# A decoder trunk on one core: score levels as two 64-column tiles, convolution taps dealt out anew, modulation sums behind each step's evacuation

## What is computed

```python
def step(state, inp):                       # recurrence, chunk by chunk
    diff = b_[:, :, :, None, :] - b_[:, :, None, :, :]
    decay = jnp.where(causal, jnp.exp(jnp.where(causal, diff, 0.0)), 0.0)
    scores = jnp.einsum('bhtk,bhsk,bhtsk->bhts', q_, k_, decay)
    o_intra = jnp.einsum('bhts,bhsv->bhtv', scores, v_)
...
u = ca * jax.nn.sigmoid(cb)
u = lax.conv_general_dilated(u, kern, window_strides=(1,), padding=[(CONV_WIDTH - 1, 0)], ...) + conv_b
u = jax.nn.silu(_layernorm(u, ln_g, ln_b))
...
mod = c_act @ w_ada[l] + b_ada[l]
sh1, sc1, g1, sh2, sc2, g2 = jnp.split(mod, 6, axis=-1)
```

## Time and profile before

| | |
|---|---|
| median of 3 runs | 927.81 us (926.43 to 931.58) |
| the profiled execution | 930.0 us, its span 928.2 us |
| TensorE busy | 846.8 us, 91% of the span |
| VectorE busy | 481.9 us, 52% |
| ScalarE, GpSimd busy | 201.9 us, 209.8 us |
| mean granted TensorE clock | 0.956 of full speed |

### The profile page before, as it was taken

How to read it: one execution, slowest core, us unless ns; L and a number is a source line. 1 busy time by engine, 2 the same in 40 slices (tenths; PEclk the granted TensorE clock), 3 DMA queues, 4 the chain that set the end, 5 groups by cost and what they waited for, 6 DMA issues and landing times.

```text
span 928.2 us, 13485 instructions
## 1 busy us (share of the span) xinstructions
PE 846.8 (91%) x5320; PEld 626.6 (68%) x5320; DVE 481.9 (52%) x608; ACT 201.9 (22%) x260; POOL 209.8 (23%) x214
## 2 busy tenths in 40 slices
PE   2799999999999999979999898799999979999970
PEld 0478899988799878768787697675555535555530
DVE  3543898896578975857999546611111101111116
ACT  4341211213331125522232242200000000000012
POOL 0000402121713110342344331012222212222220
PEclk9899999999989999998999999679999999999995
DMA  8913231112121121166675848959599999999316
GB/s 313 356 48 111 70 111 60 58 46 91 46 91 47 46 91 46 46 221 233 228 243 188 299 152 304 395 200 395 196 396 391 393 399 400 346 391 355 143 37 271
DMA packets 102313, 191.55 MB, mean 206 GB/s; under 512 B 4259, under 2 KB 41395, under 8 KB 102269
## 3 DMA queue, kind: packets, MB, share of 16 engines
q1 hardware_dynamic: 89150, 160.79, 48.0%
q10 hardware_dynamic: 9168, 19.40, 6.0%
q0 software_dynamic: 3952, 10.76, 3.2%
HBM read 182.55 MB, written 10.49 MB: 208 GB/s over the span
## 4 chain that ended last, share of the span: by engine, by line
PE 73%; DVE 11%; DMA 5%; SPq 4%; issue 4%; ACT 2%; DVEq 0%; POOL 0%; POOLq 0%; ACTq 0%
PE proj L842 16%; PE proj L558 11%; PE proj L560 11%; PE proj L559 11%; PE ha L878 8%; DVE ada_acc L1422 5%; PE pp L651 5%; SPq L450 3%; DMA ada_p<-in_w_ada 2%; DMA w_raw<-in_w_in 2%; PE pp L815 1%; DMA ew<-in_w_gate 1%; PE pp L832 1%; SPq L469 1%; PE ha L718 1%
## 5 line engine op out<-in xcount | busy, mean ns | idle before, releaser
L842 PE MATMUL proj<-ew,heT 128*64 128x256 f32 x1536 | 176.8, 383 | 6.2 <-DMA ew<-in_w_gate 3.2
L842 PEld LDWEIGHTS proj<-ew,heT 128*64 128x64 f32 x1536 | 108.5, 138 | 73.2 <-issue 17.6
L558 PE MATMUL proj<-h_hi,w_hi 128*128 128x512 f32 x368 | 147.3, 400 | 8.6 <-DVE h_lo L1205 7.2
L560 PE MATMUL proj<-h_hi,w_lo 128*128 128x512 f32 x368 | 144.3, 392 | 0.0
L559 PE MATMUL proj<-h_lo,w_hi 128*128 128x512 f32 x368 | 144.3, 392 | 0.0
L1727 POOL TENSOR_TENSOR w_lo<-w_raw,w_hi 128x2048 fp32r<-128x2048 f32 x15 | 71.1, 4743 | 103.0 <-ACT w_hi L923 103.0
L878 PE MATMUL ha<-ew,aT 128*64 128x512 f32 x384 | 87.9, 599 | 1.6 <-DVE aT L1662 0.9
L558 PEld LDWEIGHTS proj<-h_hi,w_hi 128*128 128x128 f32 x368 | 69.7, 190 | 27.9 <-issue 13.6
L923 ACT ACTIVATE w_hi<-w_raw 128x2048 fp32r<-128x2048 f32 x36 | 68.7, 1909 | 79.7 <-PE proj L560 52.4
L1326 DVE SCALAR_TENSOR_TENSOR acc<-u_t,cols_t,acc 128x512 f32<-128x512 f32 x120 | 85.4, 772 | 0.0
L560 PEld LDWEIGHTS proj<-h_hi,w_lo 128*128 128x128 f32 x368 | 69.6, 189 | 14.9
(11 more groups left out here) (244 smaller groups left out, 1317.0 us busy)
## 6 DMA issues: line engine op xcount, KB each, us to landing
ew<-in_w_gate SPq DMA_DIRECT2D x32, 1024.0 KB, 13.0
ew<-in_w_up SPq DMA_DIRECT2D x32, 1024.0 KB, 14.9
ew<-in_w_down SPq DMA_DIRECT2D x32, 1024.0 KB, 13.2
w_raw<-in_w_in SPq DMA_DIRECT2D x28, 1024.0 KB, 5.1
ada_p<-in_w_ada ACTq DMA_DIRECT2D x16, 1024.0 KB, 5.4
ada_w<-in_w_ada SPq DMA_DIRECT2D x8, 1024.0 KB, 13.3
w_raw<-in_w_o_hgrn SPq DMA_DIRECT2D x4, 1024.0 KB, 5.0
w_raw<-in_w_out SPq DMA_DIRECT2D x4, 1024.0 KB, 8.0
```

The source lines that it names most:

```text
L558: pe.matmul(outap, a_hi, b_hi, start=first, stop=False)
L560: return pe.matmul(outap, a_lo, b_hi, start=False, stop=last)
L842: mm = pe.matmul(out_ps[JS * i:JS * i + JS, 0:FG], heT[:, c_, JS * j_:JS * j_ + JS], w[:, k, FG * i:FG * i + FG], start=(kb == 0), stop=(k ...
```

## The change

`level` makes, at levels 1 to 6, two matmuls for each unit, one for each half of its 128 positions: 64 keys (48 at level 5, 32 at level 6) as weights by 32 queries. The outputs of the halves lie in partitions 0 to 63 and from 64 on of the same bank. Level 7 is as before. The masked copy becomes two of 64 partitions, on 512 elements each.

The taps are dealt out anew: 5 a step from step 4 to 11 (none before in 4 to 7, 4 in 8 to 11), 4 in 12 to 15 (as before), 3 in 16 to 23 (before 5), 4 in 24 to 31 (before 3 in 24 to 27 and none behind), 2 in 32 to 35 and 1 in 36 to 39 (before 5). The first 20 taps are the first five of each channel tile in turn, so that they depend on each other.

On VectorE a modulation half stands at the end of its step and not ahead of its evacuation, and the 16 steps are 50, 52, 54 to 58, 60 to 62, 64 to 66, 68 to 70 (before 52, 54 to 58 and so on up to 71). The first load is issued at step 44 and not 48, the second at 48, and each later one in the step behind the half that frees its buffer. GpSimd zeroes `ada_acc` at step 44 and not 47; SP waits for that ahead of the bias row, with the loads of the chunks of steps 56 and 58 behind it.

```diff
--- before.py
+++ after.py
@@ -406,7 +406,10 @@
         POOL_SPLITS = [steps[at_step[z]][2] + 1 for z in (("q", 4), ("q", 6), ("gb", 6))]
         POOL_SPLITS += range(gn, len(chunks))
 
-        taps = {(0, 8): 0, (8, 16): 4, (16, 24): 5, (24, 28): 3, (28, 32): 0, (32, 40): 5}
+        tap_order = [(w, ct) for ct in range(CT) for w in range(5)]
+        tap_order += [(w, ct) for w in range(5, CW) for ct in range(CT)]
+        tap_at = {tap: i for i, tap in enumerate(tap_order)}
+        taps = {(4, 12): 5, (12, 16): 4, (16, 24): 3, (24, 32): 4, (32, 36): 2, (36, 40): 1}
         conv_upto, total_taps = {}, 0
         for (s0, s1), n in taps.items():
             for q in range(s0, s1):
@@ -415,8 +418,10 @@
         assert total_taps == CW * CT
         merged_steps = [at_step[("ya", i)] for i in range(8)]
 
-        ADA_AT = [52, 54, 55] + [q for q in range(at_step[("ga", 0)], at_step[("ya", 7)] + 1) if q % 4 != 3]
-        ADA_AT.append(at_step[("ya", 7)])
+        ADA_AT = [50, 52, 54, 55] + [q for q in range(at_step[("ga", 0)], at_step[("ya", 7)]) if q % 4 != 3]
+        ADA_LOAD = {44: [0], 48: [1]}
+        for g in range(2, 16):
+            ADA_LOAD.setdefault(ADA_AT[g - 2] + 1, []).append(g)
         assert len(ADA_AT) == 16, len(ADA_AT)
         row_step = at_step[("ya", 7)]
         place(row_step, ("row", 0))
@@ -645,11 +650,19 @@
                     pe.wait_ge(s_ku, NLEV * qd + l - 1)
                 else:
                     pe.wait_ge(s_k, 4 * qd + 4)
-                keys = P - m if m >= 16 else P
-                for u in range(NUNIT):
-                    h, c = u // TT, u % TT
-                    mm = pe.matmul(pp[0:keys, 64 * u:64 * u + 64], k_t[:, h, P * c:P * c + keys],
-                                   tblk(q_t[:, h, P * c:P * c + P], m, 1), start=True, stop=True)
+                if m == P // 2:
+                    for u in range(NUNIT):
+                        h, c = u // TT, u % TT
+                        mm = pe.matmul(pp[0:m, 64 * u:64 * u + 64], k_t[:, h, P * c:P * c + m],
+                                       q_t[:, h, P * c + m:P * c + P], start=True, stop=True)
+                else:
+                    keys = 64 - m if m >= 16 else 64
+                    for u in range(NUNIT):
+                        h, c = u // TT, u % TT
+                        for j in range(2):
+                            t0 = P * c + 64 * j
+                            mm = pe.matmul(pp[64 * j:64 * j + keys, 32 * u:32 * u + 32], k_t[:, h, t0:t0 + keys],
+                                           tblk(q_t[:, h, t0:t0 + 64], m, 1), start=True, stop=True)
                 mm.then_inc(s_lvl, 1)
 
...
@@ -1017,8 +1030,10 @@
                 wa = w_ada[0].rearrange("(k p) n -> p k n", p=P)
                 if g >= 2:
                     act.wait_ge(s_aa, 4 * (g - 1))
+                elif g:
+                    act.wait_ge(s_ol, 2 * QH)
                 else:
-                    act.wait_ge(s_ol, 2 * QH)
+                    act.wait_ge(s_x3, 2)
                 col = 2 * D + T * (g // 2)
                 act.dma_start(ada_p[g % 2][:, :, :], wa[:, 4 * (g % 2):4 * (g % 2) + 4, col:col + T]).then_inc(s_ap[g % 2], 16)
 
@@ -1068,9 +1083,8 @@
                 evacuate(s, kind, tile, n, t)
                 for what in SLOT.get(s, ()):
                     item(what)
-                for g in range(16):
-                    if s == (ADA_AT[g - 2] if g >= 2 else 48):
-                        ada_load(g)
+                for g in ADA_LOAD.get(s, ()):
+                    ada_load(g)
...
@@ -1314,7 +1328,7 @@
 
                 while conv_at[0] < min(upto, CW * CT):
                     i = conv_at[0]
-                    w, ct = i // CT, i % CT
+                    w, ct = tap_order[i]
                     src = u_t[:, ct, w:w + T]
                     tap = cols_t[:, C_CW + CW * ct + w:C_CW + CW * ct + w + 1]
                     if w == 0:
@@ -1322,7 +1336,7 @@
                         dve.tensor_scalar(acc[:, ct, :], src, tap, cols_t[:, C_CB + ct:C_CB + ct + 1],
                                           ALU.mult, ALU.add).then_inc(s_cv, 1)
                     else:
-                        dve.wait_ge(s_cv, i - CT + 1)
+                        dve.wait_ge(s_cv, tap_at[(w - 1, ct)] + 1)
                         dve.scalar_tensor_tensor(acc[:, ct, :], src, tap, acc[:, ct, :],
                                                  ALU.mult, ALU.add).then_inc(s_cv, 1)
                     conv_at[0] += 1
@@ -1341,12 +1355,21 @@
                     m = 1 << (l - 1)
                     dve.wait_ge(s_lvl, 8 * qd + l + 1)
                     dve.wait_ge(s_st, 8 * qd + l)
-                    dst = st_t[:, :, :].rearrange("p u (b two m) -> p u b two m", two=2, m=m)[:, :, :, 1, :]
                     if l == 1 and qd == 0:
                         dve.wait_ge(s_par2, 16)
-                    msk = mask_t[:, 64 * (l - 1):64 * l].rearrange("p (o b m) -> p o b m", o=1, m=m)
-                    dve.copy_predicated(dst, msk.broadcast_to([P, NUNIT, 64 // m, m]),
-                                        pp[:, :].rearrange("p (u b m) -> p u b m", u=NUNIT, m=m)).then_inc(s_st, 1)
+                    if m == P // 2:
+                        dve.copy_predicated(st_t[0:m, :, m:P],
+                                            mask_t[0:m, 64 * (l - 1):64 * l].rearrange("p (o n) -> p o n", o=1).broadcast_to([m, NUNIT, m]),
+                                            pp[0:m, :].rearrange("p (u n) -> p u n", u=NUNIT)).then_inc(s_st, 1)
+                    else:
+                        for j in range(2):
+                            half = slice(64 * j, 64 * j + 64)
+                            dst = st_t[half, :, half].rearrange("p u (b two m) -> p u b two m", two=2, m=m)[:, :, :, 1, :]
+                            c0 = 64 * (l - 1) + 32 * j
+                            msk = mask_t[half, c0:c0 + 32].rearrange("p (o b m) -> p o b m", o=1, m=m)
+                            ins = dve.copy_predicated(dst, msk.broadcast_to([64, NUNIT, 32 // m, m]),
+                                                      pp[half, 0:512].rearrange("p (u b m) -> p u b m", u=NUNIT, m=m))
+                        ins.then_inc(s_st, 1)
 
                     if l == 1:
                         dve.wait_ge(s_fd, 4 * qd + 4)
@@ -1430,9 +1453,6 @@
             for s, (kind, tile, n, t) in enumerate(steps):
                 if t == 0 and 1 < n + 1 < NCH and n + 1 not in POOL_SPLITS:
                     split_lo(n + 1)
-                for g, at_ in enumerate(ADA_AT):
-                    if at_ == s:
-                        ada_half(g)
                 if s - 1 in merged_steps[:-1]:
                     merged_lo(steps[s - 1][1])
                 evacuate(s, kind, tile, n, t)
@@ -1444,6 +1464,9 @@
                     item(what)
                 if s in conv_upto:
                     conv(conv_upto[s])
+                for g, at_ in enumerate(ADA_AT):
+                    if at_ == s:
+                        ada_half(g)
...
@@ -1756,7 +1779,7 @@
                     evacuated(pool, at_step[("og", 4 * qd + h)])
                     pool.wait_ge(s_or, QH * qd + h + 1)
                     pool.tensor_tensor(o_t[:, h, :], o_t[:, h, :], og_t[:, h, :], ALU.mult).then_inc(s_oo, 1)
-                if (1, QH - 1) in O_NORM.get(s, ()):
+                if s == 44:
                     pool.wait_ge(s_cl, CT)
                     pool.memset(ada_acc[:, :, :], 0.0).then_inc(s_az, 1)
```

## The result

| | before | after |
|---|---|---|
| median of 4 runs | 929.38 us (926.43 to 931.58) | 914.72 us (913.45 to 917.71) |
| the profiled execution | 930.0 us, span 928.2 | 917.7 us, span 915.8 |
| ratio, with its 95% interval | | 0.985 (0.981 to 0.989) |

A fourth run of the kernel before, 930.96 us, puts its median at 929.38 where the three runs ahead of the prediction had 927.81. The change makes the kernel 14.7 us faster. The forecast was 30.4 us faster, 897.4 us with a range of 892 to 911: the sign is right, the size is half, and the time lies outside the range.

The account below looks back on a forecast made before the run. The prediction took TensorE to set the pace in the token mixer, with VectorE close behind. Savings of 18.1 + 6.4 + 1.0 + 4.9 = 30.4 us from 927.8 gave 897.4 us, range 892 to 911.

Parts of the forecast that it names:

- part 3: Modulation sums rearranged: shorter TensorE waits from step 52 to `rows_part`, 6.4 + 1.0 + 4.9 us saved.
- Part 1: Levels 1 to 6 of both quads: 64 records at 26 ns, 1.8 us a level, 18.1 us saved (14.5 to 20.5).
- 63 ns a record: Rival at the levels: records take 63 ns as at level 7, a level 4.1 us, 925 us in all; chance 0.07.
- a low clock: Rival: the clock falls behind each level, 1.6 us each, 19.6 us over twelve, 917 us in all; chance 0.05.
- The rival of halves in turn: Rival at the levels: weight loads don't run beside the other half's matmul, 82 ns a record, 939 us; chance 0.06.
- Room on VectorE: Levels 1 to 6: VectorE has 40.3 us of work in 44.4 us, 91%, so no wait is expected.
- Part 2: Taps moved to VectorE's idle time: no cost in steps 4 to 31; up to 3 us if cover in 30 and 31 fails.
- The `yb` stall: Steps 52 and 53: TensorE's wait for an evacuation behind a modulation half and the low clock after, 6.4 us saved (4 to 7.3).
- Steps 56 to 71: TensorE's idle time there, 1.5 us: evacuations no longer wait for a half, 1.0 us saved (0 to 1.5).
- `rows_part`: TensorE's wait there for the last modulation half and its slow records, priced 5.4 us: 4.9 us saved (2 to 5.4).
- Part 3 gives nothing: Rival: another load or split holds an evacuation or `rows_part` as long as now, 910 us; chance 0.11.
- token mixer ends less than 20 us earlier: End of the token mixer: a sign that, if seen, would show the forecast wrong.

Follow-up runs that it names:

- halves_in_turn: The full change with each level's 32 half matmuls reordered, all lower halves first and then all upper ones; 932.2 us, ratio 1.003 to the kernel before.
- levels_only: The kernel before with only the edits of `level` and of the masked copy, taps and modulation sums as before; 934.3 us, ratio 1.004.
- taps_moved: The full change with the taps of steps 28 to 31 moved into the levels of the second quad; 909.2 us, ratio 0.976.
- levels_taps: The kernel before with the levels and taps of the change, modulation sums as before; 917.6 us, ratio 0.986.
- ada_and_splits: The kernel before with the modulation part and all GpSimd splits on VectorE, levels and taps as before; 918.6 us, ratio 0.986.
- best_old_ada: best_a with the modulation sums as before the change; 913.6 us, ratio 0.979.
- best_a: The full change with all GpSimd splits on VectorE and the taps of steps 28 to 31 moved into the second quad's levels; 901.3 us, ratio 0.969.
- best_b: best_a with the loads of modulation halves 2 and 4 issued one step later; 897.8 us, ratio 0.967.

## Why the prediction was half right

The prediction has two failed steps. It put nothing into the sum for the taps in steps 24 to 31, and that cost 6.5 us; and it put 12.3 us there for part 3, which gave 2.9. Both have one main cause: VectorE's operations were priced by rows in which nothing runs on GpSimd beside them, or with a small part of the delay, while four of them beside GpSimd's operations took up to 6 us more.

- **Part 1, right.** Forecast 18.1 us, measured 16.9 (2 x 8.44 in the distance from level 1 to level 7). The matrix work itself fell by 39.7 - 21.3 = 18.4 us, and that this is so near is in part luck: a record at levels 1 to 4 takes 31 ns and not 26, and at levels 5 and 6 it takes 24 and 18 ns, which had been held at 24 or more, so two errors cancel. What lies between a level and the next is 155.24 - 147.31 - 1.99 = 5.94 us, 0.13 more than before. Neither the wait of 63 ns a record nor a low clock came. The rival of halves in turn was a real mechanism; it was priced at 82 ns a record and 939 us, and halves_in_turn shows 57 ns and 932.2. The change avoids it by the order of its loop.
- **Room on VectorE, right.** 91% forecast and 92% measured. levels_only shows how narrow this was.
- **Part 2, wrong.** For steps 4 to 11 "Cost nothing" holds nearly: in after TensorE waits once from 60 to 140 us, for 0.5 us. For steps 24 to 31 the sum had nothing either, and it cost 6.5 us in stretch B, and 5.5 us by the medians of taps_moved and after. The step that failed is the price of four taps, 2.7 us, which is that of taps that run alone; beside GpSimd's operations four took 5.89 and 8.75, 9.2 us more in two steps, and step 32 could not start in time, because the evacuation of step 30 stood behind them. The forecast named the place ("up to 3 us late") and the sign that it had failed, a new wait for a bank in steps 24 to 33. It put 3 us on it where 6.5 were lost: TensorE waits 3.8 us for the bank, and the mean granted clock from 253.5 to 263.5 us, around it, is 0.66.
- **Part 3, mechanism right and size wrong.** Forecast 6.4 + 1.0 + 4.9 = 12.3 us, measured 2.9 behind levels_taps and 4.4 alone. Term by term, from the trace of after:
  - The `yb` stall, 6.4: the first half was ready and short, as forecast. But the half of step 52 was held up by 4.2 us where the forecast allowed 2, the bank of step 53 came 3.2 us late and not 1, and in the 6 us at a low clock behind it 14 matmuls ran instead of 26. The stall cost 7.3 us and still costs 3.2 + 12 x 0.228 = 5.9: 1.4 saved. It was moved, not taken away.
  - Steps 56 to 71, 1.0: TensorE's waits there were 1.36 us and are 2.85, now for `w_lo`: 1.5 lost.
  - `rows_part`, 4.9: a wait of 2.0 and records of 3.70 us, where it was 3.4 and 5.40: 3.1 saved.
  
  These add up to 3.0 us. The step that failed is to price an operation from rows with nothing beside it; the rows of before had the stall twice, 5.14 us and 4.38 us, and they were taken for single cases. Part 3 gives 12.2 and 12.3 us when the splits leave GpSimd (ada_and_splits, best_old_ada). That this is the forecast sum to the tenth is luck: the kernels that it is measured against have other waits than before (2.6 us for `mb` and 4.9 at `rows_part`, not 4.8 and 3.4).
- **The rivals.** "Part 3 gives nothing" (910 us) was nearest. What happened is close to that rival together with a cost of part 2 to which no case gave more than 3 us, and this sum lies outside the range. The mark "token mixer ends less than 20 us earlier" was met: 552.74 - 539.56 = 13.2 us at the first `h_t`.

## What to carry to other kernels

Work dealt to the idle time of an engine must be priced beside what runs on its neighbour at that time: in these kernels a VectorE operation of two SBUF inputs ended 0.55 us behind the GpSimd split beside it, whenever it had begun, so 2.3 us of work moved from GpSimd to VectorE can make VectorE earlier. Edits to one resource don't add up: shorter levels without fewer taps beside them were worth nothing, and so was moving the splits without rearranging the halves; all together, with no taps in steps 28 to 31, they brought 28 to 32 us (best_a, best_b). Count an engine's work step by step over the whole stretch that gets more, not in one step of it.
